# Dealing a vector engine's modulation sums out in smaller portions between the tiles of a gated in-projection

## The reference

```python
cs = jax.nn.silu(c)
for l in range(2):
    mod = cs @ mod_w[l] + mod_b[l]                    # 1024 -> 6 * 1024
    sh1, sc1, g1, sh2, sc2, g2 = jnp.split(mod, 6, axis=-1)
    h = rmsnorm(x, norm_mix_g[l]) * (1 + sc1) + sh1
    y = conv_lru_mixer(h, ...) if l % 2 == 0 else dilated_attn_mixer(h, ...)
    x = x + g1 * y
    h = rmsnorm(x, norm_ffn_g[l]) * (1 + sc2) + sh2
    x = x + g2 * grouped_moe(h, ...)                  # 16 experts, top 2
return rmsnorm(x, final_norm_g)
```

```python
z = h @ w_in                                # 1024 -> 2560: a_val, a_gb, a_gc, b_gate, b_in
y_a = a_gb * depthwise_conv(a_gc * a_val)
xr = depthwise_conv(b_in) + bias
h_rec = rglru(xr, forward) + rglru(xr, backward)   # gates by 64x64 blocks, then a scan over time
y_b = gelu(b_gate) * h_rec
out = concatenate([y_a, y_b]) @ w_out
```

## Time and profile before

| | |
|---|---|
| median of 3 runs | 1404.65 us (1403.72 to 1407.47) |
| the profiled execution | 1405.48 us, of which the profile's span is 1403.7 us |
| PE busy | 1262.3 us (90%) |
| DVE busy | 1040.5 us (74%) |
| ACT busy | 677.9 us (48%) |
| mean granted TensorE clock | 0.95 |
| in-projection in the trace | 40.8 to 204.95 us |
| out-projection in the trace | from 205.78 us |

### The profile page before, as it was taken

The page is one execution under the profiler, slowest core; times in us unless marked ns, Lnnn a source line. Parts: engine busy times, 40 slices in busy tenths (PEclk is TensorE's granted clock), DMA queues, the critical chain, the costliest instruction groups (busy, mean ns, idle before and its releaser), DMA issues.

```text
span 1403.7 us, 15168 instructions
## 1 busy us (share of the span) xinstructions
PE 1262.3 (90%) x5185; PEld 886.2 (63%) x5185; DVE 1040.5 (74%) x1443; ACT 677.9 (48%) x859; POOL 162.8 (12%) x169
## 2 busy tenths in 40 slices
PE   2999899949999999987999999999499999999886
PEld 2466665537777777743788854467377777777432
DVE  8678885477988888836766587856678898888253
ACT  3476401326676666613322167734276667666002
POOL 6000000010000000011000057710100000000200
PEclk9999899869999999999999999999599999999999
DMA  9637665256999999894365330022679999998641
GB/s 353 235 93 261 229 240 211 90 209 255 378 380 384 386 384 393 318 366 151 112 248 180 90 121 1 1 76 110 261 287 391 388 382 383 381 385 320 244 173 60
DMA packets 78115, 347.82 MB, mean 248 GB/s; under 512 B 12500, under 2 KB 12684, under 8 KB 69104
## 3 DMA queue, kind: packets, MB, share of 16 engines
q1 hardware_dynamic: 67184, 325.70, 61.8%
q0 software_dynamic: 7344, 16.68, 3.4%
q10 hardware_dynamic: 3536, 4.79, 0.9%
HBM read 334.15 MB, written 23.07 MB: 254 GB/s over the span
## 4 chain that ended last, share of the span: by engine, by line
PE 74%; DVE 14%; ACT 4%; DMA 4%; issue 3%; POOL 0%; SPq 0%; DVEq 0%; ACTq 0%; POOLq 0%
PE ps L1939 24%; PE ps L2062 8%; PE ps L1965 8%; PE ps L1972 6%; PE ps L1859 4%; PE ps L1930 3%; DVE scratch L1044 3%; PE ps L1866 3%; PE ps L1925 2%; PE ps L1826 2%; PE ps L2106 2%; PE ps L2134 2%; PE ps L2120 2%; DMA x_res<-in_x_dram 1%; PE ps L1821 1%
## 5 line engine op out<-in xcount | busy, mean ns | idle before, releaser
L1939 PE MATMUL ps<-slab_ring_r,gate_rows_r 128*128 128x512 f32 x512 | 201.7, 394 | 0.0
L1466 DVE TENSOR_TENSOR slab_ring_r<-slab_ring,h_t_r 128x2048 fp32r<-128x2048 f32 x64 | 143.8, 2285 | 5.6 <-ACT h_t_r L857 5.6
L2062 PE MATMUL ps<-slab_ring_r 128*128 128x512 f32 x384 | 122.1, 399 | 4.1 <-DVE h_t_r L1101 4.1
L857 ACT ACTIVATE h_t_r<-slab_ring 128x2048 fp32r<-128x2048 f32 x64 | 118.8, 1904 | 0.0
L1939 PE MATMUL ps<-h_t_r,gate_rows_r 128*128 128x512 f32 x256 | 105.6, 412 | 12.2 <-issue 7.3
L1965 PE MATMUL ps<-slab_ring,scratch 128*128 128x512 f32 x256 | 115.2, 593 | 1.5 <-ACT scratch L897 1.5
L1939 PEld LDWEIGHTS ps<-slab_ring_r,gate_rows_r 128*128 128x128 f32 x512 | 97.7, 191 | 18.6
L1939 PE MATMUL ps<-h_t_r,scratch_r 128*128 128x512 f32 x256 | 101.9, 398 | 0.0
L724 POOL TENSOR_SCALAR mod_ring<-mod_ring,row_rcp 128x512 f32<-128x512 f32 x48 | 77.0, 1617 | 206.2 <-DVE row_rcp L1712 206.2
L1466 DVE TENSOR_TENSOR slab_ring_r<-slab_ring,mod_ring_r 128x2048 fp32r<-128x2048 f32 x32 | 73.1, 2288 | 19.3 <-ACT mod_ring_r L857 19.3
L1466 DVE TENSOR_TENSOR slab_ring_r<-slab_ring,x_norm_r 128x2048 fp32r<-128x2048 f32 x32 | 73.1, 2288 | 18.3 <-ACT x_norm_r L857 18.3
(11 more groups left out here) (357 smaller groups left out, 2675.6 us busy)
## 6 DMA issues: line engine op xcount, KB each, us to landing
slab_ring<-in_expert_w_gate_dram SPq DMA_DIRECT2D x35, 2048.0 KB, 9.8
slab_ring<-in_expert_w_up_dram SPq DMA_DIRECT2D x35, 2048.0 KB, 10.0
slab_ring<-in_expert_w_down_dram SPq DMA_DIRECT2D x35, 2048.0 KB, 10.1
mod_ring<-in_mod_w_dram SPq DMA_DIRECT2D x40, 512.0 KB, 4.7
y_rows<-scratch SPq DMA_DIRECT2D x32, 512.0 KB, 10.6
slab_ring<-in_mod_w_dram SPq DMA_DIRECT2D x32, 512.0 KB, 4.6
slab_ring<-in_mod_w_dram SPq DMA_DIRECT2D x12, 1024.0 KB, 11.3
slab_ring<-in_w_qkv_dram SPq DMA_DIRECT2D x6, 2048.0 KB, 11.8
```

Source lines behind the costliest of these rows:

```text
L857: act.activation(top, w, ACT.Copy).then_inc(high_ready[c], 1)
L1466: tt_(rest, w, top.bitcast(F32), ALU.subtract).then_inc(low_ready[c], 1)
L1939: ins = pe.matmul(ps[:, bank, :], x, w, start=(kt == 0 and i == 0), stop=(kt == KT - 1 and i == 2))
L2062: ins = pe.matmul(ps[:, i % 6, :], x[:, kt, cut], y[:, k, :], start=(kt == 0 and n == 0), stop=(kt == KT - 1 and n == 2))
```

## The change

The same additions, loads and reductions are made, in another order. On DVE the portions of `mod_acc` become pairs up to the fourth scan, and each part ends later. Six pieces of part 6 come after `gb(3)`. The reductions of parts 2, 3 and 4 come after tiles 9, 14 and 17 instead of 8, 11 and 15, and that of part 5 moves into the out-projection's first row tile. On SP the slabs 3 and 4 of `w_in` and half 0 of `w_out` stand further up among the pieces' loads.

```diff
@@ block.sync
         load_mod(2, range(4, MOD_SLICES))
-        load_mod(3)
+        load_mod(3, range(4))
         sp.wait_ge(z_ready, 4)
         load_slab(("out", 0), w_out[:, :, 0:HALF])
         sp.wait_ge(z_ready, 8)
         load_in(3)
-        load_mod(4)
+        load_mod(3, range(4, MOD_SLICES))
+        load_mod(4, range(4))
         load_in(4)
+        load_mod(4, range(4, MOD_SLICES))
         load_mod(5)
         sp.wait_ge(z_ready, 12)
         load_slab(("out", 1), w_out[:, :, HALF:D])
@@ block.vector
         conv_b(3)
-        mod_acc(2, 0, 3)
+        mod_acc(2, 0, 2)
         gates_in(0)
-        mod_acc(2, 3, 3)
+        mod_acc(2, 2, 2)
         gates_out(0)
         low_in(2, 0)
-        mod_acc(2, 6, 2)
+        mod_acc(2, 4, 2)
         low_in(2, 1)
         gates_in(1)
-        mod_acc(3, 0, 3)
+        mod_acc(2, 6, 2)
         gates_out(1)
+        mod_acc(3, 0, 2)
+        gates_in(2)
         mod_take(2)
-        mod_acc(3, 3, 3)
-        gates_in(2)
-        mod_acc(3, 6, 2)
+        mod_acc(3, 2, 2)
         gates_out(2)
         low_in(3, 0)
-        mod_acc(4, 0, 3)
+        mod_acc(3, 4, 2)
         gates_in(3)
-        mod_acc(4, 3, 2)
+        mod_acc(3, 6, 2)
         gates_out(3)
         low_in(3, 1)
-        mod_acc(4, 5, 3)
+        mod_acc(4, 0, 3)
         mod_take(3)
         val(0)
-        mod_acc(5, 0, 3)
+        mod_acc(4, 3, 3)
         val(1)
         low_in(4, 0)
-        mod_acc(5, 3, 3)
+        mod_acc(4, 6, 2)
         val(2)
-        mod_acc(5, 6, 2)
+        mod_acc(5, 0, 3)
         val(3)
         mod_take(4)
         low_in(4, 1)
-        mod_acc(6, 0, 3)
+        mod_acc(5, 3, 3)
         gb(0)
-        mod_acc(6, 3, 3)
+        mod_acc(5, 6, 2)
         gb(1)
-        mod_acc(6, 6, 2)
+        mod_acc(6, 0, 2)
         gb(2)
         gb(3)
+        mod_acc(6, 2, 6)
         mod_take(5)
@@ block.tensor
-        reduce_after = {8: 2, 11: 3, 15: 4, 18: 5}
+        reduce_after = {9: 2, 14: 3, 17: 4}
@@ experts(l), block.tensor
                 project(l, t, 0, 3, 6)
+                if l == 0 and t == 0:
+                    mod_reduce(MOD_SPLIT - 3)
                 if t:
                     logits(t - 1)
                 project(l, t, 0, 6, KT)
```

## The result

The changed kernel takes 1415.72 us (median of 4 runs, 1413.96 to 1416.5) against 1404.54 us before: a ratio of 1.0074, with an interval of 1.006 to 1.0088. Its profiled execution took 1416.29 us, its span is 1414.5 us.

What follows compares the result with a forecast made beforehand. PE, 90% busy, was taken as the bound, with in-projection tiles waiting for DVE's low_in. A lag of 9.1 at the out-projection plus 1.7 gave +10.8 us: 1404.65 + 10.8 = 1415.5, range 1411.5 to 1418.5.

Steps and rivals of the forecast that it cites:

- Step 1: Up to tile 12: fewer pieces ahead and slab 3 no longer late, a gain of 3.4 us.
- Step 2: Tile 14: ACT's gates of block 3 held only by the third scan, a gain of 4.5 us.
- Steps 3 and 4: DVE waits for reductions 3 and 4 before their takes, delaying tiles 16 and 18: losses of 6.7 and 4.9 us.
- step 4: DVE waits 4.8 us for reduction 4, tiles 16 and 17 taking 7.2 + 5.45; tile 18 lags 7.1 us.
- Step 5: Before the out-projection: part 6's first piece lands late behind the output slab, costing 1.5 us; lag becomes 9.1.
- rival B: Part 6's piece is there in time, passing the slab or because DVE comes later: +9.3 to +6.7 us; chance 0.15.
- Step 6: Out-projection: reduction 5 moves into its first row tile, 1.7 us more; six pieces and the take cost nothing.
- The clock: Unknown clock at the out-projection's start after 2.3 us idle PE: taken as high, cost 0; low would cost about 1.7 us.
- Rival C: The clock falls once more at the out-projection: +12.5 us, 1417.2; chance 0.13.
- Rival D: Not slower: the wait of mod_take costs nothing, PE's own work follows tile 14: 1402.1 us; chance 0.08.

Runs made afterwards that it cites:

- experiment 5: The kernel before with only the changed kernel's list of loads, engine orders as before: 1400.78 us against 1404.74, ratio 0.9976.
- experiment 1: The changed kernel with reduction 3 after tile 13 instead of tile 14: 1406.3 us, ratio 1.0008 to the kernel before.
- experiment 2: The changed kernel with DVE's take of part 3 moved from before val(0) to behind low_in(4, 0): 1409.52 us, ratio 1.0037.
- experiment 7: The changed kernel with reductions 3 and 4 after tiles 13 and 16 instead of 14 and 17: 1404.06 us, ratio 0.9997.
- experiment 3: The changed kernel with half 1 of the output weights loaded ahead of part 5 instead of behind it: 1415.73 us, ratio 1.0079.
- experiment 6: The kernel before with only six pieces of part 6 behind gb(3) and reduction 5 in the first out-projection row tile: 1403.93 us, ratio 0.9993.
- experiment 4: The changed kernel with the list of loads of the kernel before: 1437.12 us, ratio 1.0232.
- experiment 8: The changed kernel with reductions 3 and 4 after tiles 13 and 16 and output weights' half 1 loaded ahead of part 5: 1401.25 us, ratio 0.9976.

## Why the prediction was right

Every step is found in the trace, in its order, with these times:

| step | forecast | measured |
|---|---|---|
| 1: tile 8, tile 12 | 101.3, 138.9 | 100.30, 138.01 |
| 2: tile 14 | 156.9 | 156.13 |
| 3: wait before the take of part 3; tile 16 | 7.7; 179.9 | 7.88; 179.41 |
| 4: wait before the take of part 4; tile 18 | 4.8; 199.1 | 5.13; 199.00 |
| 5: the late piece lands after; out-projection | 9.1; 214.9 | 9.2; 214.71 |
| 6: reduction 5 in the out-projection | 1.7 | 1.72 |

**Step 1.** Slab 3 was issued at 111.3 and was there when ACT came for it at 127.2. The time of 100.30 for tile 8 is 1.0 earlier than forecast for a reason outside the change: the executions of this study that share this order up to tile 8 have it between 99.9 and 101.6. Counted from tile 8, the out-projection comes 114.4 us later, not 113.6. The 0.8 us are spread over the stretches between the tiles (0.1, 0.1, 0.3, 0.4 and -0.1). Two small misses thus cancelled in the total, and the rest of the kernel happened to agree to 0.2 us. So the agreement of 11.2 with 10.8 is partly luck; that of the steps, taken one by one, is not.

**Step 2.** ACT's gates of block 3 began at 134.8 behind the scan. Experiment 5 has the list of loads alone, and gains 3.7 us in the trace.

**Steps 3 and 4** were the cause of most of the loss, and it is shown, not argued: experiment 1 takes away the first wait by moving the reduction, experiment 2 by moving the take, and they bring back 9 and 6 of the 11 us. Experiment 7 takes both waits away and the loss is nil. Of the 9 us of experiment 1 about 2 are the clock: behind the shorter wait tiles 16 and 17 run 1.9 us faster. The prediction had this inside step 4, where it gave tile 16 the low clock for the pause ahead of it.

**Step 5** had its mechanism and size right: the pause before the out-projection was 2.25 us where 0.83 stand without the late piece (experiment 3), so 1.4 for the 1.5 of the forecast. The landing behind the slab was 9.2 us, and rival B, a piece that passes the slab, did not happen. What this lateness costs in the whole time is shown only beside experiment 7 (2.8 us, part of it the clock); on the changed kernel itself (experiment 3) the time did not move.

**Step 6.** Reduction 5 took the 1.72 us, and the additions beside it cost nothing; experiment 6 confirms that the tail is neutral.

**The clock.** The idle time before the out-projection was 2.25 us, near the 2.3 expected, and its products stayed at full clock. That choice had less ground than I gave it, and that it came out was luck. I went by the length of the pause, 2.41 us high and 2.77 low. In experiment 1 a pause of 1.85 us was followed by slow products (7.08 instead of 5.39 us) and in experiment 4 one of 1.96 us (7.08 too), in experiment 2 one of 2.57 us was not. The length of the last pause does not decide it. Rival C was thus nearer than its 0.13, and it would have been inside the range.

The page "TensorE: Matmul & The Clock Gate" of the Trainium skill (Part 1) says that the monitor behind the clock runs freely against the program. The runs fit this in that the start of the out-projection met both levels (experiments 1 and 2). But these are two kernels with one trace each; no run shows it within one kernel, nor the monitor itself.

Rival D did not happen as the change stands, but its mechanism did in experiment 7: 1404.06 us, against D's 1402.1, with the late piece still in it.

## What to carry to other kernels

When additions are moved on one engine, move the reduction that another engine makes of them and the take that waits for it as a group. A take that waits holds up everything queued behind it for its whole wait, and one place in TensorE's order (after tile 13, not 14) was worth 9 us of 11. Look for the idle gap that the producer has anyway: here a 3.6 us reduction was free in the 5.3 us before tile 14. Try the parts of a change alone: here the new list of loads by itself (experiment 5, 0.9976) gave as much as the whole new order with its reductions and slab put right (experiment 8, 0.9976). And check each shared list of loads for what is newly behind a late use: a 2 MB slab there made the next 512 KB load land after 9.2 us, where one alone took 4.5.

## What was unexpected of the hardware

The granted clock at the start of the out-projection did not follow the length of the pause before it: 1.85 us of idle PE and slow products in experiment 1, 1.96 and slow in experiment 4, 2.83 and slow in experiment 7, but 2.25 and 2.57 and full clock in the changed kernel and experiment 2. The time of the first 12 products was 5.39, 7.08 or 8.46 us accordingly. This alone is 1.7 to 3.1 us in kernels that differ by single waits, and may be why experiment 1's runs spread over 1403.28 to 1409.37 us; that last point was not tested.

Slow products came without any pause too. In the changed kernel and in experiment 2 tile 15 ran slow right behind a column reduction, 16 products of one column in 3.6 us at full clock, with no idle time in between (granted 0.51 from 166.9 to 169.9 us in the changed kernel).
